# The feed-forward norm moved into the expert block, piece by piece with the first query products, its low halves on POOL

## The reference

```python
def rmsnorm(x, w):
    y = x32 * lax.rsqrt(jnp.mean(x32 * x32, axis=-1, keepdims=True) + RMS_EPS)
    return (y * w.astype(jnp.float32)).astype(x.dtype)
def modulate(h, shift, scale):
    return h * (1 + scale) + shift
x = x + g_m * y_l
x = x + g_f * peer_ffn(modulate(rmsnorm(x, norm_ffn_w[i]), sh_f, sc_f), ...)
# peer_ffn, per block of 128 tokens
q = (xc @ w_q).reshape(PEER_BLOCK, PEER_HEADS, 2, PEER_KEY_DIM // 2)
s = jnp.einsum("chsd,hskd->chsk", q, keys)
top_s, top_i = lax.top_k(s, PEER_TOPK)
...
act = jax.nn.gelu(jnp.einsum("cd,chkd->chk", xc, u_tab[e]))
return jnp.einsum("chk,chkd->cd", g * act, v_tab[e])
```

## Time and profile before

| | |
|---|---|
| median of 3 runs | 2988.3 us (2984.59 to 2992.66) |
| the profiled execution | 2994.03 us, span 2992.2 us |
| granted TensorE clock, mean | 0.946 of full speed |
| busy: PE, DVE, ACT, POOL | 88%, 70%, 24%, 44% of the span |
| DMA | 917.85 MB, mean 307 GB/s |
| first layer's feed-forward norm begins | 394.39 us |
| second layer's | 1782.72 us |

### The profile page before, as it was taken

How to read it: one execution, slowest core, us unless ns; L and a number is a source line. 1 busy time by engine, 2 the same in 40 slices (tenths; PEclk the granted TensorE clock), 3 DMA queues, 4 the chain that set the end, 5 groups by cost and what they waited for, 6 DMA issues and landing times. The chain is left out here.

```text
span 2992.2 us, 36261 instructions
## 1 busy us (share of the span) xinstructions
PE 2635.3 (88%) x12550; PEld 2170.5 (73%) x12550; DVE 2087.3 (70%) x4563; ACT 707.4 (24%) x1947; POOL 1322.6 (44%) x1060
## 2 busy tenths in 40 slices
PE   4789869999999999999946878999999999999991
PEld 2544557888888888788844756788888887888881
DVE  2365249989979856666674346998988975666667
ACT  2345142224434300000004424213444410000000
POOL 0000014455667755555650003354557764755653
PEclk7889989999999999999977988999999999999995
DMA  7156133799999999999991213598999999999995
GB/s 298 64 212 270 50 110 123 268 356 363 372 363 409 409 404 409 409 409 409 409 362 63 77 57 128 185 351 323 381 357 401 409 409 405 409 409 409 409 409 200
DMA packets 246589, 917.85 MB, mean 307 GB/s; under 512 B 27120, under 2 KB 32272, under 8 KB 239120
## 3 DMA queue, kind: packets, MB, share of 16 engines
q0 software_dynamic: 147456, 536.94, 45.9%
q1 hardware_dynamic: 94800, 374.54, 32.6%
q10 hardware_dynamic: 4160, 4.19, 0.4%
HBM read 909.27 MB, written 6.29 MB: 306 GB/s over the span
## 5 line engine op out<-in xcount | busy, mean ns | idle before, releaser
L1177 PE MATMUL exp_down<-peer_gates,all_ring 128*128 128x256 f32 x2720 | 615.5, 382 | 28.0 <-DMA all_ring<-in_peer_v 27.4
L1149 PE MATMUL exp_out<-peer_hd,all_ring 128*128 128x256 f32 x2752 | 619.8, 382 | 11.1 <-DMA all_ring<-in_uT 6.8
L1177 PEld LDWEIGHTS exp_down<-peer_gates,all_ring 128*128 128x128 f32 x2720 | 508.3, 190 | 125.5 <-DMA all_ring<-in_peer_v 59.2
L1149 PEld LDWEIGHTS exp_out<-peer_hd,all_ring 128*128 128x128 f32 x2752 | 519.5, 191 | 89.9 <-DMA all_ring<-in_uT 15.1
L1098 POOL DMA_INDIRECT all_xT<-in_u_rows,peer_eidx x284 | 367.4, 1294 | 180.7 <-DVE peer_dots L1521 111.5
L1528 DVE SCALAR_TENSOR_TENSOR peer_hs<-all_xT,peer_dots,peer_hs 128x1024 f32<-128x1024 f32 x224 | 287.8, 1285 | 153.1 <-DMA all_xT<-in_peer_v,peer_eidx 143.7
L1071 POOL TENSOR_TENSOR ask_w_lo<-all_ring,ask_w_hi 128x1024 fp32r<-128x1024 f32 x22 | 52.3, 2390 | 725.6 <-ACT ask_w_hi L1205 725.6
L1521 DVE CUSTOM_DVE_ANT_0 all_xT<-all_xT,peer_hs 128x1024 f32<-128x1024 f32 x284 | 343.8, 1220 | 28.7 <-DMA all_xT<-in_u_rows,peer_eidx 26.8
L1098 POOL DMA_INDIRECT all_xT<-in_peer_v,peer_eidx x228 | 256.7, 1126 | 196.5 <-DVE peer_hs L1528 168.0
L1177 PE MATMUL exp_down<-peer_gates,spare_ring 128*128 128x256 f32 x1376 | 314.4, 381 | 9.8 <-DMA spare_ring<-in_peer_v 9.8
L1149 PE MATMUL exp_out<-peer_hd,spare_ring 128*128 128x256 f32 x1344 | 306.7, 381 | 6.1 <-DMA spare_ring<-in_uT 3.0
(11 more groups left out here) (292 smaller groups left out, 3848.8 us busy)
## 6 DMA issues: line engine op xcount, KB each, us to landing
all_ring<-in_uT SPq DMA_DIRECT2D x172, 512.0 KB
all_ring<-in_peer_v SPq DMA_DIRECT2D x170, 512.0 KB
mix_raw<-in_ada_tiles SPq DMA_DIRECT2D x48, 1024.0 KB, 10.2
spare_ring<-in_peer_v SPq DMA_DIRECT2D x86, 512.0 KB
spare_ring<-in_uT SPq DMA_DIRECT2D x84, 512.0 KB
all_ring<-in_w_peer_q SPq DMA_DIRECT2D x22, 512.0 KB, 3.9
all_ring<-in_w_gs_in SPq DMA_DIRECT2D x16, 512.0 KB, 3.7
all_ring<-in_w_in SPq DMA_DIRECT2D x12, 512.0 KB, 3.7
```

What stands on the lines that cost most here:

```text
L1149: mm = nc.tensor.matmul(outs[:, c % 2, 0:DENSE], raw[c % R][:, k, :], hd[:, k, :], start=(k == 0), stop=(k == KD - 1))
L1177: mm = nc.tensor.matmul(dn[:, m, :], raw[at % R][:, m, :], gates[:, :, c, :], start=(c == 0 and m % 2 == 0), stop=(c == NKEYS - 1), skip_g ...
```

## The change

The separate norm phase ahead of the expert block is gone, and with it one barrier. Its steps are written into the queues of the expert block:

- ACT squares, then splits the first two weight tiles, then takes the root. For each piece it applies only the shift, over all 512 columns at once, first into `both` (which holds `hs` and `hd`), then once more from the same source into `hi`.
- DVE multiplies stream, gain and reciprocal in one operation into four buffers (`scaled`). It makes no low halves any more.
- POOL makes the eight low halves, 512 columns each, between its first and its second weight split.
- TensorE's first query product waits piece by piece for them. The transposes stand behind it, and the scores of m = 0 directly behind these, ahead of the second product. The fourth block's score has its own semaphore and, for m = 0, follows the second product.
- SP issues the first three weight tiles, the keys and the copy of the stream at the start of the block, which is now the start of the norm.
- The norm's tiles lie where the block's second half of gate values will be written later. `norm_phase` loses its option `halves`.

```diff
--- before.py
+++ after.py
@@ -911,6 +895,12 @@
+        norms = Lay(nc, f"norm{l}", at + half, 54 * P * 4)
+        self.square = norms.sb("square", [P, KD, SEQ])
+        self.rstd = norms.sb("rstd", [P, SEQ])
+        self.gain = norms.sb("gain", [P, KD])
+        self.scaled = [norms.sb(f"scaled{j}", [P, 2, PICKED]) for j in range(4)]
@@ -1022,16 +1014,20 @@
+        total = ps_t[:, 1, :]
...
@@ -1041,9 +1037,8 @@
-            for j in range(2):
-                sp.sem_inc(s_w[j], 16)
-            sp.dma_start(asked[2][:, :, :], w[2]).then_inc(s_w[2], 16)
+            for m in range(3):
+                sp.dma_start(asked[m][:, :, :], w[m]).then_inc(s_w[m], 16)
@@ -1099,7 +1094,16 @@
-            for m in range(HS):
+            def low(k):
+                pool.wait_ge(s_moved, k + 1)
+                nc.gpsimd.tensor_tensor(lo[:, k, :].rearrange("p (b n) -> p b n", b=2), both[:, :, k, :],
+                                        f32(hi[:, k, :]).rearrange("p (b n) -> p b n", b=2),
+                                        ALU.subtract).then_inc(s_low, 1)
+
+            split_lo(0)
+            for k in range(KD):
+                low(k)
+            for m in range(1, HS):
                 split_lo(m)
@@ -1109,19 +1113,31 @@
-            for b in range(FETCHED):
-                for k in range(KD):
-                    mm = nc.tensor.transpose(turned[b][:, k * P:(k + 1) * P], hs[:, k, b * P:(b + 1) * P], ident[:, :])
-            mm.then_inc(s_rows, 1)
+            for i in range(KD // 2):
+                pe.wait_ge(s_pair, i + 1)
+                mm = nc.tensor.matmul(total, ones[:, :], q.square[:, 2 * i, :], start=(i == 0), stop=(i == KD // 2 - 1))
+            mm.then_inc(s_sum, 1)
             def ask(m):
                 pe.wait_ge(s_lo, m + 1)
                 if m >= 2:
                     pe.wait_ge(s_q, m - 1)
                 for k in range(KD):
+                    if m == 0:
+                        pe.wait_ge(s_low, k + 1)
                     mm = three_passes(nc, query[m % 2], q.w_hi[m % 3][:, k, :], q.w_lo[m % 3][:, k, :],
                                       hi[:, k, :], lo[:, k, :], k == 0, k == KD - 1)
                 mm.then_inc(s_asked, 1)
+
+            def turn_rows():
+                for b in range(FETCHED):
+                    for k in range(KD):
+                        mm = nc.tensor.transpose(turned[b][:, k * P:(k + 1) * P], hs[:, k, b * P:(b + 1) * P],
+                                                 ident[:, :])
+                mm.then_inc(s_rows, 1)
...
@@ -1129,17 +1145,27 @@
                 pe.wait_ge(s_q, m + 1)
                 if m >= 2:
                     pe.wait_ge(s_top, TOPS * (m - 2) + 3 * LATER)
+                for b in range(LATER):
+                    mm = score_block(m, b, scores[m % 2][:, b, :])
+                mm.then_inc(s_score, 1)
+
+            def later_score(m):
+                if m == 0:
+                    pe.wait_ge(s_own, 1)
+                if m >= 2:
                     pe.wait_ge(s_held, m - 1)
-                for b in range(NB):
-                    to = scores[m % 2][:, b, :] if b < LATER else later[m % 2]
-                    mm = nc.tensor.matmul(to, q.qT[m % 3][:, b * P:(b + 1) * P], q.keys[:, m, :], start=True, stop=True)
-                mm.then_inc(s_score, 1)
+                score_block(m, LATER, later[m % 2]).then_inc(s_later_score, 1)
             ask(0)
-            for m in range(HS):
+            turn_rows()
+            score(0)
+            ask(1)
+            later_score(0)
+            for m in range(1, HS):
                 if m + 1 < HS:
                     ask(m + 1)
                 score(m)
+                later_score(m)
             def up(c):
                 pe.wait_ge(s_in[c % R], 16 * (c // R + 1))
@@ -1205,21 +1231,34 @@
                 act.activation(q.w_hi[m % 3][:, :, :], asked[m % 3][:, :, :], ACT.Copy).then_inc(s_hi, 1)
             def hold(m):
-                act.wait_ge(s_score, m + 1)
+                act.wait_ge(s_later_score, m + 1)
                 act.activation(q.later_scores[:, m, :], later[m % 2], ACT.Copy).then_inc(s_held, 1)
+            for k in range(KD):
+                act.activation(q.square[:, k, :], xT[:, k, :], ACT.Square).then_inc(s_square, 1)
             split_hi(0)
             split_hi(1)
+            act.wait_ge(s_sum, 1)
+            act.activation(q.rstd[:, :], total, ACT.Sqrt, bias=eps[:, 0:1], scale=1.0 / D).then_inc(s_std, 1)
+            for k in range(KD):
+                act.wait_ge(s_scaled, k + 1)
+                act.activation(both[:, :, k, :], q.scaled[k % 4][:, :, :], ACT.Identity, bias=norm_shift[:, k:k + 1])
+                act.activation(hi[:, k, :].rearrange("p (b n) -> p b n", b=2), q.scaled[k % 4][:, :, :], ACT.Identity,
+                               bias=norm_shift[:, k:k + 1]).then_inc(s_moved, 1)
             split_hi(2)
-            act.wait_ge(s_rows, 1)
-            for b in range(FETCHED):
-                for h in range(2):
-                    act.activation(own[:, b, h * 512:(h + 1) * 512], turned[b][:, h * 512:(h + 1) * 512], ACT.Copy)
             for m in range(HS):
                 act.wait_ge(s_asked, m + 1)
                 if m >= 3:
                     act.wait_ge(s_score, m - 2)
+                    act.wait_ge(s_later_score, m - 2)
                 act.activation(q.qT[m % 3][:, :], query[m % 2], ACT.Copy).then_inc(s_q, 1)
+                if m == 0:
+                    act.wait_ge(s_rows, 1)
+                    for b in range(FETCHED):
+                        for h in range(2):
+                            last = act.activation(own[:, b, h * 512:(h + 1) * 512], turned[b][:, h * 512:(h + 1) * 512],
+                                                  ACT.Copy)
+                    last.then_inc(s_own, 1)
                 if m + 3 < HS:
                     split_hi(m + 3)
                 if m >= 1:
@@ -1528,6 +1567,23 @@
                     nc.vector.scalar_tensor_tensor(out=acc[:, b, :], in0=row, scalar=q.dots[:, b, k:k + 1],
                                                    in1=acc[:, b, :], op0=ALU.mult, op1=ALU.add).then_inc(s_used, 1)
+            for i in range(KD // 2):
+                dve.wait_ge(s_square, 2 * i + 2)
+                nc.vector.tensor_tensor(q.square[:, 2 * i, :], q.square[:, 2 * i, :], q.square[:, 2 * i + 1, :],
+                                        ALU.add).then_inc(s_pair, 1)
+            nc.vector.tensor_scalar(q.gain[:, :], norm_scale, 1.0, None, ALU.add).then_inc(s_gain, 1)
+            dve.wait_ge(s_gain, 1)
+            nc.vector.tensor_tensor(q.gain[:, :], q.gain[:, :], norm_weight, ALU.mult).then_inc(s_gain, 1)
+            dve.wait_ge(s_std, 1)
+            nc.vector.reciprocal(q.rstd[:, :], q.rstd[:, :]).then_inc(s_rstd, 1)
+            dve.wait_ge(s_rstd, 1)
+            dve.wait_ge(s_gain, 2)
+            for k in range(KD):
+                if k >= 4:
+                    dve.wait_ge(s_moved, k - 3)
+                nc.vector.scalar_tensor_tensor(out=q.scaled[k % 4][:, :, :].rearrange("p b n -> p (b n)"),
+                                               in0=xT[:, k, :], scalar=q.gain[:, k:k + 1], in1=q.rstd[:, :],
+                                               op0=ALU.mult, op1=ALU.mult).then_inc(s_scaled, 1)
             dve.wait_ge(s_spill, 32)
             for m in range(HS):
                 top16(m)
@@ -1651,12 +1707,10 @@
                 gemm_phase(nc, "gsout", ring, t["w_gs_out"], KD, hi, lo, SEQ, take_dve=residual(nc, xT, mod(1, G_M)))
             ffn_w = small[:, ROW_FFN + l * KD:ROW_FFN + (l + 1) * KD]
             with Room(nc, f"peer{l}") as pr:
-                hs = pr.sb("hs", [P, KD, PICKED])
-                hd = pr.sb("hd", [P, KD, DENSE])
-                norm_phase(nc, f"nffn{l}", xT, SEQ, ffn_w, mod(l, SH_F), mod(l, SC_F), hi, lo, ones, eps,
-                           ring=ring, next_w=t["w_peer_q"][l], halves=(hs, hd))
+                both = pr.sb("both", [P, 2, KD, PICKED])
                 q = Experts(nc, pr, l, split_at)
-                peer_phase(nc, t, l, xT, x_dram, hi, lo, ring, hs, hd, ident, iota_b, mod(l, G_F), q)
+                peer_phase(nc, t, l, xT, x_dram, hi, lo, ring, both,
+                           (ones, eps, ffn_w, mod(l, SH_F), mod(l, SC_F)), ident, iota_b, mod(l, G_F), q)
         with Room(nc, "final") as fr:
             y = fr.sb("y", [P, KD, SEQ])
```

More of the change, by code:

```diff
@@ L268, in _, with norm_phase @@
             dve.wait_ge(mods.s_taken, mods.FIRST)
-def norm_phase(nc, tag, src, n, weight, shift, scale, hi, lo, ones, eps, plain=None, ring=None, next_w=None, halves=None):
+def norm_phase(nc, tag, src, n, weight, shift, scale, hi, lo, ones, eps, plain=None, ring=None, next_w=None):
     with Room(nc, tag) as r:
@@ L278, in norm_phase @@
         normed = [r.sb(f"normed{j}", [P, n]) for j in range(S)]
-        modded = [r.sb(f"modded{j}", [P, n]) for j in range(S)] if halves is None else None
+        modded = [r.sb(f"modded{j}", [P, n]) for j in range(S)]
```

(7 more changed lines are left out.)

36 lines of the change are left out of this document (11 added, 25 removed).

## The result

The changed kernel takes **2961.7 us** (median of 4 runs, 2961.1 to 2962.6); the kernel before, on the same chip, 2987.5. The ratio is 0.9911, with an interval from 0.9898 to 0.9923. So it is faster by some 26 us. I had forecast 2973.0 with a range down to 2966: the direction was right, the size and the range were not. The profiled executions stand 32.8 us apart in their spans. The two layers, which carry the change, make up 15.6 and 12.5 of that. Another 3.0 lie ahead of the first feed-forward norm and are no part of the change: other kernels of this study with nothing altered there start that norm anywhere between 389.6 and 394.0 us.

What follows compares the result with a forecast made beforehand. It took the chain before the fetches as what counts, with DVE the bound from 463 to 600 us. Layers gaining 7.3 and 8.1 us sum to 15.4, from a 2988.3 median to 2973.0; range 2966 to 2985.

Steps and rivals of the forecast that it cites:

- Steps (1) to (7): Chain from the norm's squares to the third query product: that product starts 7.3 us sooner (first layer), 8.1 (second).
- Step (8): The rest of the layer: barrier already counted, earlier transfers and extra semaphores change nothing; sum of both layers 15.4 us.
- only 7.3 count: DVE's first top-16 work starts 12 us sooner, but the next scores need the third product, which moves 7.3 us.
- It is the bound there: Query part, 463 to 600 us: DVE bounds it, never waiting over 1 us, but starts each time from TensorE's scores.
- now three go first and the fourth follows the second product, so that sum stays: Step (6), scores after the transposes: four blocks took 0.81 us before, and the new order leaves the sum unchanged.
- Rival B: Norm: DVE's scalings and POOL's low halves hinder each other, 3.7 us a layer, 7.4 both, giving 2980.4; chance 0.09.
- step (5): TensorE's first query product follows POOL's low halves piece by piece, ending at 419.9 instead of 430.48: 10.6 us sooner.
- step (4): POOL's norm low halves take 1.30 us each; the rule favouring VectorE would make it 1.1 us a layer better.
- Rivals A: Norm start: second weight tile lands late, delaying ACT's root to 408.1; two layers lose 12 us, leaving 2985; chance 0.08.
- C: After 463 us: DVE or the DMA engines hold a fixed date and absorb the shift, giving 2988; chance 0.08.
- D: Norm: POOL's low half is dear, at 3.2 us each giving 3003, slower than before; chance 0.05.

Runs made afterwards that it cites:

- experiment 5: Kernel before, with DVE told of a piece's scores after the three blocks it searches instead of all four: 2977.7 us, ratio 0.9946.
- experiment 2: Changed kernel, with POOL subtracting 4 columns instead of 1024 for the weights' low halves from the fourth piece on: 2960.4 us, ratio 0.9905 to before.
- experiment 1: Kernel before, with POOL subtracting 4 columns instead of 1024 for the weights' low halves from the fourth piece on: 2973.5 us against 2990.2, ratio 0.9938.
- experiment 6: Changed kernel, with DVE's search of every piece but the first waiting for the fourth block's score too: ratio 0.9956 to before.
- experiments 3: Changed kernel, with POOL making each low half of the weights twice from the fourth piece on: 3001.3 us, ratio 1.0041 to before.
- experiment 7: Changed kernel, with the norm's eight low halves on DVE, each two pieces behind its scaling, none on POOL: ratio 0.9897 to before.

## Why the prediction was wrong, step by step

- **Steps (1) to (7), the chain of the norm: right.** Root at 7.48 us after the squares (7.5 said). In the second layer it came at 7.53 instead of 6.2. ACT waited for TensorE there: the last sums over channels took 0.59 to 1.06 us each, where in the second layer of before they took 0.59 to 0.70, so TensorE was at its lower clock for them. That is no effect of the change: the same kernel run again had its root at 6.21, and the kernel of experiment 5, with the norm of before, at 7.55. Third product at 34.96 (35.2 said). Two errors cancelled. The first product ended at 26.8 us, not 25.5, as the low halves came at 1.6 to 1.7 us apart for the first five, then at 1.24. The 16 transposes took 1.74 us, not 2.8, as the clock was already up. The third product of the second layer came 7.1 us sooner, where I had 8.1. Experiments 2 and 5 measure this chain by itself at the last product: 7.5 us (between 1 and 2) and 7.7 (between 5 and after) in the first layer, where I had 7.3, and 8.3 and 7.7 in the second, where I had 8.1.
- **Step (8), "only 7.3 count", and its ground in the first part, "It is the bound there": wrong.** I took DVE for the bound since it never waited. But busy there held 11.5 us of standing still in the first layer (2.1, 2.1, 0.45 and 6.85 us in four instructions), and it made TensorE wait. Experiment 5 shows what failed: the line about the scores ("now three go first and the fourth follows the second product, so that sum stays") counted matmuls and not the time at which DVE is told. That step was worth 16 us in before (ratio 0.9946) and, taken back in after, 13 (0.9956 against 0.9911). In the two profiled layers the account is this: 14.6 us at the third product (15.4 said), 12.0 more up to the last product (nothing said; experiment 5 alone has 11.0 of this kind), and 1.5 in the stage behind, together 28.1, against 26 in the medians.
- **Rival B, 0.09: its mechanism was true.** I had argued against it that POOL's subtractions keep their length "whether DVE works or idles". That row could not show it: where the two meet it is mostly DVE that stands still. The Trainium skill, "GPSIMD Engine Reference", section "1. Specifications", which I had cited for this rival, was the better guide: it names DVE instructions with two SBUF inputs, and also those in a 2-port perf mode. The addition of experiment 6 (6.94 us) has two inputs and agrees. The stopped instructions shown for experiments 3 and 6 with 2.39 and 2.34 us have one; in which mode they ran stands in no row. In the norm the price was about what it said in kind and less in size: the low halves came 1.3 us late against step (5), not 3.7.
- **The rule weighed in step (4)**, that such work belongs on VectorE: by experiment 7 the product chain would gain 2.7 us from it in the first layer and 3.0 in the second, where I had 1.1, but the time of the kernel did not show it.
- **Rivals A, C and D: not seen.** No tile was late, the shift reached the end of both layers, and no low half took more than 1.75 us.
- **The range** had no case below 2966, as all my cases were prices of the chain; none was an interference elsewhere that the change could remove.

Open: why the stage behind the last product takes 1042 to 1049 us in the first layer and 1042 to 1054 in the second. It moved by up to 7.4 us with no edit at all (the kernel run again), so that experiment 7's 2.7 us did not arrive need not have a cause in that kernel. In the other comparisons with before this stage has a share too: 7.6 of the 19.5 us by which experiment 1's two layers are shorter, 4.1 of the 15.2 of experiment 5. I made no run on it. What is shown for the stops is their effect up to the last product.

## What to carry to other kernels

Do not take an engine that never waits for the bound before comparing the length of each of its instructions with the shortest of the same form: a copy of 64 columns that takes 2.3 us is a wait in disguise. Where POOL works on tensors beside a DVE chain, a shift of a fraction of a microsecond can decide whether they collide, and a first collision can bring others behind it (11.5 us of standing still in the first layer of before, 2.2 in experiment 5); such a shift may be had by signalling a result as soon as the part that is needed is there. And a gain on the engine that is not the bound, as in experiment 2, need not reach the end: about half of it was handed back at the next wait, and the time of the kernel showed nothing of it.

## What the runs showed of the hardware that I had not expected

- Many DVE instructions from SBUF to SBUF that start during a POOL subtraction of 1024 columns stand still until all POOL subtractions queued without a break are over: 2.29 us under one, 7.02 under three (4.74 and 2.39 long). One that starts 0.08 us ahead of POOL takes its 0.19. Most that started 0.00 to 0.02 us behind POOL still got through; 0.04 us behind was enough to be stopped (the addition at 485.17 in after, 4.76 us, behind POOL's start at 485.13).
- It goes by the form. Over all the runs, all 24 two-input operations on 32 float32 columns and all 10 copies of 64 columns that started in such a subtraction were stretched. None of 61 copies of 96 columns (uint32 to bf16) was, each at its 0.25 us. No search was either (MAX8, FIND_INDEX8, MATCH_REPLACE8), as at 468.47. Why the copies differ is not shown.
- A 512-column pair on either side (experiment 7) slows both instead: 1.70 for 1.28 and 1.26 for 0.75 in the median.
- The price of a short wait of TensorE is more than the wait. In experiment 6 the scores behind a wait of 3.94 us took 1.62 us for six matmuls instead of 0.83. In before, with one wait of 3.90 us and a granted clock of 0.95 over the 70 us, the last product ended 6.3 us later than in experiment 5.
